# Depthwise convolution taps on TensorE: five tiles in four position phases instead of four tiles in two

## The reference

```
h = rms_norm(x, norm_g)
u = h @ pw1_w + pw1_b
u = u[..., :D_MODEL] * sigmoid(u[..., D_MODEL:])
u = causal_depthwise_conv(u, dw_w, dw_b)      # 31 taps for each of 1024 channels
u = silu(layer_norm(u, ln_g, ln_b))
return x + u @ pw2_w + pw2_b
```

## Time and profile before

| | us |
|---|---|
| median of 3 runs (1230.75 to 1232.16) | 1231.62 |
| the profiled execution | 1231.28 |
| its span | 1229.5 |
| TensorE busy | 1201.1 (98%) |
| VectorE busy | 788.4 (64%) |
| ScalarE busy | 504.6 (41%) |
| first projection ends on TensorE | 98.99 |
| last band matmul ends | 159.96 |

### The profile page before, as it was taken

One profiled execution on the slowest core, in us unless ns is written; L12 is line 12 of the kernel. 1 busy time (PEld: TensorE's weight loads), 2 busy tenths in 40 slices (PEclk: granted clock), 3 DMA queues, 4 the chain that ended last, 5 costly groups with the idle time before them and its releaser, 6 DMA issues.

```text
span 1229.5 us, 16391 instructions
## 1 busy us (share of the span) xinstructions
PE 1201.1 (98%) x6106; PEld 1009.4 (82%) x6106; DVE 788.4 (64%) x1083; ACT 504.6 (41%) x814; POOL 61.4 (5%) x76
## 2 busy tenths in 40 slices
PE   8999969999999999999999999999899999999998
PEld 6888748888888888887999999887688888888887
DVE  6997955577537762676467667765577437753664
ACT  6332154544214431335565656553434224332441
POOL 1000001100000000002212111100000000000000
PEclk9999989999999999999999999998999999999999
DMA  8554702233322232323321222221222323332322
GB/s 296 143 127 114 205 26 69 69 103 102 103 97 78 99 110 96 103 65 107 103 70 35 70 70 69 69 70 35 69 83 88 127 79 103 101 104 69 102 77 94
DMA packets 34614, 116.77 MB, mean 95 GB/s; under 512 B 18304, under 2 KB 18432, under 8 KB 21888
## 3 DMA queue, kind: packets, MB, share of 16 engines
q1 hardware_dynamic: 34560, 116.03, 30.0%
HBM read 109.60 MB, written 6.49 MB: 94 GB/s over the span
## 4 chain that ended last, share of the span: by engine, by line
PE 91%; DVE 5%; ACT 3%; issue 1%; DMA 0%; POOL 0%; SPq 0%; ACTq 0%; DVEq 0%
PE bank L1229 70%; PE bank L1385 9%; PE bank L1302 5%; PE bank L1450 2%; PE bank L1419 1%; DVE w_lo L834 1%; PE bank L1323 1%; PE bank L1293 1%; PE bank L1268 1%; PE bank L1404 1%; DMA w_raw<-stream 0%; ACT prob L788 0%; DVE w_lo L826 0%; ACT xg_hi L568 0%; ACT w_hi L561 0%
## 5 line engine op out<-in xcount | busy, mean ns | idle before, releaser
L1229 PE MATMUL bank<-xg_hi,w_hi 128*128 128x512 f32 x832 | 327.7, 394 | 6.2 <-DVE w_lo L826 3.7
L1229 PE MATMUL bank<-xg_lo,w_hi 128*128 128x512 f32 x832 | 324.3, 390 | 0.0
L1229 PE MATMUL bank<-xg_hi,w_lo 128*128 128x512 f32 x832 | 324.2, 390 | 0.0
L551 ACT ACTIVATE w_hi<-w_raw 128x2048 fp32r<-128x2048 f32 x79 | 150.7, 1907 | 151.1 <-PE bank L1229 147.1
L826 DVE TENSOR_TENSOR w_lo<-w_raw,w_hi 128x2048 fp32r<-128x2048 f32 x79 | 182.6, 2312 | 31.5 <-ACT w_hi L551 31.5
L1229 PEld LDWEIGHTS bank<-xg_hi,w_hi 128*128 128x128 f32 x832 | 156.5, 188 | 41.3 <-DVE w_lo L826 4.1
L1229 PE MATMUL bank<-act_hi,w_hi 128*128 128x512 f32 x448 | 177.1, 395 | 7.5 <-DVE act_lo L979 7.2
L1229 PEld LDWEIGHTS bank<-xg_lo,w_hi 128*128 128x128 f32 x832 | 156.6, 188 | 33.8 <-issue 1.7
L1229 PEld LDWEIGHTS bank<-xg_hi,w_lo 128*128 128x128 f32 x832 | 156.5, 188 | 32.8
L703 ACT ACTIVATE ffn_t<-ffn_u,par 128x512 f32<-128x512 f32 x88 | 72.0, 818 | 268.8 <-DVE ffn_u L1049 268.8
L1229 PE MATMUL bank<-act_lo,w_hi 128*128 128x512 f32 x448 | 175.1, 391 | 0.0
(11 more groups left out here) (160 smaller groups left out, 1448.3 us busy)
## 6 DMA issues: line engine op xcount, KB each, us to landing
w_raw<-stream SPq DMA_DIRECT2D x87, 1024.0 KB, 4.9
band_sb<-band SPq DMA_DIRECT2D x12, 512.0 KB, 7.7
w_raw<-stream SPq DMA_DIRECT2D x8, 768.0 KB, 4.2
band<-band_sb SPq DMA_DIRECT2D x4, 1056.0 KB, 12.1
x<-x_t SPq DMA_DIRECT2D x8, 256.0 KB, 6.3
w_raw<-band SPq DMA_DIRECT2D x4, 512.0 KB, 6.1
out_t<-x SPq DMA_DIRECT2D x8, 256.0 KB, 2.0
w_raw<-stream SPq DMA_DIRECT2D x2, 512.0 KB, 4.9
```

The source lines that it names most:

```text
L551: act.activation(w_hi[:, j, :], w_raw[:, j, :], ACT.Copy).then_inc(w_hi_done, 1)
L1229: got = pe.matmul(out, weights(w, j, k, m), v[:, k, :], start=(k == first and s == 0), stop=(k == last and s == 2), skip_group_check=True)
```

## The change

Three tiles (0 to 2) stay on VectorE, five (3 to 7) go to TensorE. A band now has 32 channels in four position phases: 9 offsets of four positions, 9 blocks of 128 columns (BAND_COLS = 1152), matmuls of 128 columns. There are 4 bands to a tile and 20 in all. ScalarE copies into u2 in 16 copies of 32 partitions a tile and evicts each band in four copies of 32x128. A row of the band block in DRAM has 1248 elements instead of 2112. scatter works by tile, in four transfers of 32x31 elements, and the fifth tile's comes last. Each band is one transfer: on the DRAM side 4 x 32 x 1152 elements with steps of 32, 1248 and 1, on the SBUF side 128 rows of 4608 bytes. There are 13 homes: 3 in w_raw, 3 in band_sb, and 7 over xg_hi and xg_lo, which are free when the first projection is through; SyncE waits for that (tiles). Bands 13 to 19 go to homes 3 to 9. The next units' weight loads stand between the loads of bands 12 and 13. VectorE sums tiles 0 to 6 into sq_sum in six adds (conv_summed), and TensorE makes two matmuls with ones, of that sum after band 18 and of tile 7 at the end. ScalarE splits the next units' weights behind the evictions of bands 6 and 11.

```diff
-DVE_TILES = [0, 1, 2, 3]
-PE_TILES = [4, 5, 6, 7]
-PHASES = 2
+DVE_TILES = [0, 1, 2]
+PE_TILES = [3, 4, 5, 6, 7]
+PHASES = 4
+CH = P // PHASES
+OFFSETS = (TAPS + PHASES - 2) // PHASES + 1
+BAND_COLS = OFFSETS * P
+BAND = (OFFSETS * PHASES + PHASES - 1) * CH
...
+RAW_BANDS = 3
+SB_BANDS = 3
+XG_BANDS = 7
+BAND_LOADS = 1
+HOMES = RAW_BANDS + SB_BANDS + XG_BANDS
...
+        xg_band, _ = put("xg_band", at, [P, XG_BANDS * BAND_COLS])
         xg_hi, at = put("xg_hi", at, [P, KT, SEQ], F32R)
...
         def band_slot(n):
-            return n if n < 2 else 2 + n % 2
+            return n if n < HOMES else n - HOMES + RAW_BANDS
...
             def load_band(n):
-                tile, h = divmod(n, 2)
-                for r in range(PHASES):
-                    sp.dma_start(band_home(n)[r * HD:(r + 1) * HD, :],
-                                 bass.AP(band.tensor, (tile * P + h * HD) * BAND + r * HD, [[BAND, HD], [1, SLOT]])
-                                 ).then_inc(band_in[band_slot(n)], 16)
...
+                sp.dma_start(band_home(n), bass.AP(band.tensor, n * CH * BAND, [[CH, PHASES], [BAND, CH], [1, BAND_COLS]])
+                             ).then_inc(band_in[band_slot(n)], 16)
+
+            def scatter(tile):
+                sp.wait_ge(band_zero[tile], 16)
+                for g in range(PHASES):
+                    sp.dma_start(bass.AP(band.tensor, (tile * PHASES + g) * CH * BAND + (PHASES - 1) * CH,
+                                         [[BAND + 1, CH], [CH, TAPS]]),
+                                 bass.AP(params.tensor, g * CH * N_PARAMS + PARAM_AT["dw_w"] + PE_TILES[tile] * TAPS,
+                                         [[N_PARAMS, CH], [1, TAPS]]),
+                                 allow_slow_non_contiguous=True).then_inc(band_set, 16)
...
-                    scatter((n - 2 * RING) // RING)
-
-            sp.wait_ge(band_set, 32 * len(PE_TILES))
-            for n in range(2):
-                sp.wait_ge(w_lo_done, KT - RING + n + 1)
+                    for tile in range(len(PE_TILES))[n - 2 * RING:n - RING]:
+                        scatter(tile)
+
+            scatter(len(PE_TILES) - 1)
+            sp.wait_ge(band_set, 16 * BANDS)
+            for n in range(RAW_BANDS):
+                sp.wait_ge(w_lo_done, KT - RING + 1 if n == 0 else KT)
                 load_band(n)
-            load_band(2)
-            load_band(3)
-            for n in range(4, BANDS):
-                if n in (4, 5):
-                    sp.wait_ge(band_used, n - 3)
-                    sp.dma_start(w_raw[:, n % 2, :], stream[:, STARTS[KT + n % 2]:STARTS[KT + n % 2 + 1]]).then_inc(w_in[n % 2], 16)
-                sp.wait_ge(band_used, n - 1)
+            for n in range(RAW_BANDS, RAW_BANDS + SB_BANDS):
+                load_band(n)
+            sp.wait_ge(tiles, TILE0 + 2 * KT)
+            for n in range(RAW_BANDS + SB_BANDS, HOMES):
+                load_band(n)
+            for j in range(RING):
+                sp.wait_ge(band_used, 2 + j)
+                sp.dma_start(w_raw[:, j, :], stream[:, STARTS[KT + j]:STARTS[KT + j + 1]]).then_inc(w_in[j], 16)
+            for n in range(HOMES, BANDS):
+                sp.wait_ge(band_used, band_slot(n) + 1)
                 load_band(n)
...
                 if m in PE_TILES:
-                    act.wait_ge(pad_done, 1)
-                    n = 2 * (m - PE_TILES[0])
-                    for h in range(2):
+                    act.wait_ge(pad_done, 2)
+                    n = PHASES * (m - PE_TILES[0])
+                    for g in range(PHASES):
                         for r in range(PHASES):
-                            got = act.activation(u2[r * HD:(r + 1) * HD, n + h, :],
-                                                 conv_u[h * HD:(h + 1) * HD, m, r:CP:PHASES], ACT.Copy)
+                            at = conv_u[g * CH:(g + 1) * CH, m, r:CP:PHASES]
+                            got = act.activation(u2[r * CH:(r + 1) * CH, n + g, 0:at.shape[-1]], at, ACT.Copy)
                     got.then_inc(u_split, 1)
...
                 for e in range(PHASES):
-                    got = act.activation(conv_c[h * HD:(h + 1) * HD, PE_TILES[tile], e:SEQ:PHASES],
-                                         bank[CONV[n % len(CONV)]][(1 - e) * HD:(2 - e) * HD, 0:HALF_SEQ], ACT.Copy)
+                    got = act.activation(conv_c[g * CH:(g + 1) * CH, PE_TILES[tile], e:SEQ:PHASES],
+                                         bank[CONV[n % len(CONV)]][(PHASES - 1 - e) * CH:(PHASES - e) * CH, 0:PHASE_SEQ], ACT.Copy)
                 got.then_inc(band_out, 1)
-                if n in (2, 3):
+                if n in (6, 11):
                     split_weights(KT + n % 2, n % 2)
...
+            own.mark(dve.memset(u2[:, :, PHASE_COLS - 1:PHASE_COLS], 0.0))
...
-            convolve(16)
+            convolve(len(taps))
             split_weights(KT, 0)
...
-            convolve(12)
-            split_weights(KT + 1, 1)
-            convolve(len(taps))
+            dve.wait_ge(c_done, len(DVE_TILES))
+            for n in range(KT - 2):
+                if n:
+                    dve.wait_ge(conv_summed, n)
+                if n + 1 in PE_TILES:
+                    dve.wait_ge(band_out, PHASES * (n + 2 - PE_TILES[0]))
+                if n == len(DVE_TILES) + 1:
+                    split_weights(KT + 1, 1)
+                dve.tensor_tensor(sq_sum, sq_sum if n else conv_c[:, 0, :], conv_c[:, n + 1, :], ALU.add).then_inc(conv_summed, 1)
...
                 for o in range(OFFSETS):
-                    got = pe.matmul(bank[CONV[n % len(CONV)]][:, 0:HALF_SEQ], band_home(n)[:, o * P:(o + 1) * P],
-                                    u2[:, n, o:o + HALF_SEQ], start=o == 0, stop=o == OFFSETS - 1, skip_group_check=True)
+                    got = pe.matmul(bank[CONV[n % len(CONV)]][:, 0:PHASE_SEQ],
+                                    band_home(n)[:, o * P:(o + 1) * P], u2[:, n, o:o + PHASE_SEQ],
+                                    start=o == 0, stop=o == OFFSETS - 1, skip_group_check=True)
                 got.then_inc(band_used, 1)
...
-                if h == 1:
-                    if tile < len(DVE_TILES) - 1:
-                        pe.wait_ge(c_done, tile + 1)
-                        mean(DVE_TILES[tile], start=tile == 0)
-                    if tile:
-                        pe.wait_ge(band_out, 2 * tile)
-                        mean(PE_TILES[tile - 1])
-            pe.wait_ge(c_done, len(DVE_TILES))
-            mean(DVE_TILES[-1])
+                if n == BANDS - 2:
+                    pe.wait_ge(conv_summed, KT - 2)
+                    mean(sq_sum, start=True)
             pe.wait_ge(band_out, BANDS)
-            mean(PE_TILES[-1], stop=True).then_inc(mean_mm, 1)
+            mean(conv_c[:, PE_TILES[-1], :], stop=True).then_inc(mean_mm, 1)
```

More of the change, by code:

```diff
@@ L260, in trunk @@
         ln_sq, at = put("ln_sq", at, [P, 2, SEQ])
-        band_sb, at = put("band_sb", at, [P, 2 * SLOT])
-        zeros = band_sb[:, 2 * SLOT - BAND:2 * SLOT]
+        band_sb, at = put("band_sb", at, [P, SB_BANDS * BAND_COLS])
+        zeros = band_sb[:, SB_BANDS * BAND_COLS - BAND:SB_BANDS * BAND_COLS]
         neg_mean = conv_a[:, 0, :]
@@ L330, in trunk @@
         zeros_set = sem("zeros_set")
-        band_zero = [sem(f"band_zero{n}") for n in range(2)]
+        band_zero = [sem(f"band_zero{n}") for n in range(len(PE_TILES))]
         band_set = sem("band_set")
-        band_in = [sem(f"band_in{n}") for n in range(4)]
+        band_in = [sem(f"band_in{n}") for n in range(HOMES)]
         band_used = sem("band_used")
@@ L339, in trunk @@
         mean_mm = sem("mean_mm")
+        conv_summed = sem("conv_summed")
         xc_done = sem("xc_done")
@@ L387, in band_slot @@
         def band_slot(n):
-            return n if n < 2 else 2 + n % 2
+            return n if n < HOMES else n - HOMES + RAW_BANDS
         def band_home(n):
-            return w_raw[:, n, 0:SLOT] if n < 2 else band_sb[:, (n % 2) * SLOT:(n % 2 + 1) * SLOT]
+            at = band_slot(n)
+            if at < RAW_BANDS:
+                home = w_raw.rearrange("p j c -> p (j c)")
+            elif at < RAW_BANDS + SB_BANDS:
+                home, at = band_sb, at - RAW_BANDS
+            else:
+                home, at = xg_band, at - RAW_BANDS - SB_BANDS
+            return home[:, at * BAND_COLS:(at + 1) * BAND_COLS]
         def band_count(n):
-            return 32 if n < 2 else 32 * (n // 2)
+            return 16 * BAND_LOADS * (n // HOMES + 1)
         block = ctx.enter_context(nc.Block())
@@ L410, in fill @@
             def fill(tile):
-                sp.dma_start(bass.AP(band.tensor, tile * P * BAND, [[BAND, P], [1, BAND]]), zeros).then_inc(band_zero[tile // 2], 16)
+                sp.dma_start(bass.AP(band.tensor, tile * P * BAND, [[BAND, P], [1, BAND]]), zeros).then_inc(band_zero[tile], 16)
             def load_band(n):
-                tile, h = divmod(n, 2)
-                for r in range(PHASES):
```

(22 more changed lines are left out.)

11 lines of the change are left out of this document (4 added, 7 removed).

## The result

The changed kernel takes 1295.12 us (median of 4 runs, 1294.84 to 1296.19) against 1231.74 beside it: a ratio of 1.0514, 95% interval 1.0499 to 1.0528, slower. The forecast was 1285 with a range of 1268 to 1306.

A forecast was written before the change was run, and what follows sets the result against it. TensorE bound the old kernel; four-engine band loads would bind the new: 90 + 2.4 + 20 x 5.6 + 5.0, then the tail, gives 215.3, plus 1 for variance: +53.7 on 1231.3, 1285 us; range 1268 to 1306 at 0.8.

The forecast's parts named there:

- the stall at band 3: TensorE waits 3.4 us at band 3 for the first eviction, queued behind ScalarE's 16 copies of tile 7.
- the sum: Tap stage with band transfers on four engines: start, landing, bands, weight loads and tail put the mean's takeover at 215.3.
- first band load issued: SyncE issues the first band load near 90 (87 to 92), 8 us later for the fifth tile's scatter.
- issue to landing beyond the transfer: For a band load, 2.4 us on top of its transfer, from a lone 1 MB load landing 4.9 us after issue.
- 20 bands: Band loads confined to four engines at 106 GB/s, 5.6 us each, 112 us in all.
- two weight loads: their quarter on the four engines: Two 1 MB weight loads between bands 12 and 13 need the four engines 2.5 us each, 5.0 together.
- last band to mean: After the last load: matmuls 2.0, eviction 1.3, mean 0.9, 0.2 between, plus 1.5 for low clock.
- variance: The variance matmuls behind the mean take 1 us more, some of them running at the low clock.
- Transfers on the same four queues follow one another: Band and weight loads on the DMA queues run in sequence, so homes and their waits don't matter.
- weights for the next units are in long before: Behind the mean, at 162.57 before the change, everything moves as a block, since later weights arrive early.
- the first rival: Band transfers use all 16 engines, 1.4 us a band; TensorE then bounds, 17.4 us earlier, 1214; chance 0.09.
- The 0.13 for faster: Chance that the whole changed kernel runs faster; sixteen engines at full rate had 0.09, at half rate 0.04.

The follow-up runs named there:

- the plain load: Changed kernel with each band loaded as one transfer of 128 consecutive, non-overlapping DRAM rows, so matmul operands hold other taps than wanted; 1222.95 us, ratio 0.992.

## Why the prediction was right, and where 10 us went

The chain of reasoning held at each joint: a share of 0.25 at 106 GB/s (forecast and measured), 5.57 us a band (5.6), TensorE waiting for the DMA, the stall at band 3 covered by those waits, all behind the mean moving as a block. The mean is taken over at 225.03 where the sum had 215.3. By the sum's own terms:

| term | forecast | measured | difference |
|---|---|---|---|
| first band load issued | 90 | 91.15 | +1.2 |
| issue to landing beyond the transfer | 2.4 | 4.1 (9.65 to the matmuls, less 5.57) | +1.7 |
| 20 bands | 112 | 111.4 | -0.6 |
| two weight loads: their quarter on the four engines | 5.0 | 4.9 | -0.1 |
| bands slowed beside these two loads | 0 | 3.9 | +3.9 |
| left over between bands 9 and 14 | 0 | 1.0 | +1.0 |
| bands slowed beside two more, behind band 19 in the queue | 0 | 3.7 | +3.7 |
| last band to mean | 5.9 (with the low clock) | 5.0 | -0.9 |
| variance | +1 | +1.5 | +0.5 |

The differences add up to 10.4 where 10.2 are to be explained (63.9 against 53.7); the rest is rounding. Nearly all have one sign, so the hit owes little to errors that cancel; what kept it inside the range is that the range ran to 1306. The mechanism was right and one effect was missing. The weight loads' own price, 2.5 us each on the four engines, was right. What the sum had at nothing is what the bands lose while the other twelve engines move the rest: 3.9 us at the first pair and 3.7 at the second. "Transfers on the same four queues follow one another" held for those four, and "weights for the next units are in long before" was a statement on when they are wanted, while what cost time was where they ran: beside bands 17 and 18. A load without a deadline still takes bandwidth from one that has one.

The landing term has another cause than it names. The windows from 93 to 95 and from 95 to 100 read 74 and 89 GB/s instead of 106:

```profile
93.00:95.00 2.00, 1.00 0.23 74
95.00:100.00 5.00, 3.77 (x17) 1.00 0.25 89
```

By these figures 149 KB were missing at 100, an estimate of 1.4 of the 1.7 us: the first band moved slowly, and no run shows why.

Smaller steps. ScalarE's copies (347 ns, measured 453, and 7.3 us a tile, not 5.6) and evictions (290, measured 395) fell outside what rows at steps 1 and 2 could show; hidden here by the band waits, they would have cost the first rival 2.1 us at band 3, as the plain load showed (5.5 against 3.4). TensorE caught up by band 14, not 16. Records start 112 ns apart at full clock (2.02 us for 18) against the 110 taken; ten of the twenty bands took 3.1 to 3.9 us, wholly or partly at the lower clock, also hidden. Only the last band and the means stand on the path by their own length, and those ran at full clock, so the 1.5 us set aside for the low clock weren't needed.

The 0.13 for faster belonged to sixteen engines. The runs add that even there the kernel would have gained 9 us (ratio 0.992), not 17.

## What to carry to other kernels

Read the leading count of both access patterns before pricing a transfer: the same 0.59 MB moved at 53, 106, 240 or about 400 GB/s with leading counts of 2, 4, 32 and 128, and four issues of 32 rows were far cheaper than one of 4 x 32. A load that uses a few engines leaves the others free, and here what those moved slowed it to about half. Price what else runs on the engines in the stretch where a load is the bound, whether or not anyone waits for it. And when a wait is taken away, ask which of the engine's next instructions now comes too early: here GpSimd's copies gained nothing while the split still stood ahead of the evictions.

## What the runs showed of the hardware

- Beside loads on four engines, 128-row loads of 1 MB filled a share of 1.0, and both together moved 242 GB/s, where such loads alone move 423. From 156 to 160 the loads on four engines moved 51 rows, where they move 92 in 4 us alone, and a pair of such loads cost them 3.9 us by this, and 4.9 us for its quarter on the four engines themselves.
- Of two loads issued behind others that use four engines, three quarters of the rows (192) moved from 152 to 164, before what stood ahead of them was through, and one quarter (64) from 170 to 176, behind it.
- Four transfers of 32 rows moved 228 to 247 GB/s in the order 0, 1, 2, 3 and 269 to 293 in the order 0, 2, 1, 3.
- On ScalarE a step of 4 float32 elements on either side added 0.12 us to a copy of 128 columns, steps of 2 next to nothing, and rows 32 or 128 made no difference.
- GpSimd's 16 copies of 32x136 took 13.19 us, 0.82 each, and VectorE's tap sums took 0.91 us beside them instead of 0.74, as these two lines of the kernel with GpSimd's copies show (during and after):

```profile
114.78 0.91 DVE L948 SCALAR_TENSOR_TENSOR conv_c<-conv_u,par,conv_c 128x512 f32<-128x512 f32 x1
115.61 0.74 DVE L948 SCALAR_TENSOR_TENSOR conv_b<-conv_u,par,conv_b 128x512 f32<-128x512 f32 x1
```
